# Squares kept as a pair of tiles, attention column groups on alternating PSUM halves, and a TensorE loop written out, in a decoder layer step

## The reference, cut to what matters

```python
x = x + 0.5 * swiglu(rmsnorm(x, g_ffn1), w_ffn1_in, w_ffn1_out)
h = rmsnorm(x, g_mix);  p = h @ w_in          # q, k, v of attention and GLA, gates
a  = rms(dilated_attention(...)) * g_att_out   # 16 heads x 64
gg = rms(gated_linear_attention(...)) * g_gla_out * silu(r_g)
x = x + concat(a, gg) @ w_out
x = x + 0.5 * swiglu(rmsnorm(x, g_ffn2), w_ffn2_in, w_ffn2_out)
y = rmsnorm(x, g_final)
# rmsnorm(x, g) = x * rsqrt(mean(x*x, features) + eps) * g
```

## Time and profile before

| | |
|---|---|
| median of 3 runs | 2145.38 us |
| lowest, highest | 2140.80, 2151.92 us |
| span of the profiled execution | 2142.6 us |
| PE busy | 2075.4 us, 97% |
| DVE busy | 1201.3 us, 56% |
| ACT busy | 881.7 us, 41% |
| POOL busy | 151.1 us, 7% |
| HBM traffic | 180 GB/s over the span |

### The profile page before, as it was taken

One profiled execution on the slowest core, in us unless ns is written; L12 is line 12 of the kernel. 1 busy time (PEld: TensorE's weight loads), 2 busy tenths in 40 slices (PEclk: granted clock), 3 DMA queues, 4 the chain that ended last, 5 costly groups with the idle time before them and its releaser, 6 DMA issues.

```text
span 2142.6 us, 40469 instructions
## 1 busy us (share of the span) xinstructions
PE 2075.4 (97%) x16651; PEld 2043.7 (95%) x16651; DVE 1201.3 (56%) x1300; ACT 881.7 (41%) x986; POOL 151.1 (7%) x93
## 2 busy tenths in 40 slices
PE   8999999999999999999988799999999999999997
PEld 7999999999999999999977799999999999999997
DVE  6555554554454545655698967655555545544443
ACT  5433434434343435433345534434344343433332
POOL 0000000000000001005342450000000000000000
PEclk9999999999999999999999899999999999999998
DMA  5665565665555465448975464555655555555553
GB/s 192 181 183 177 166 193 179 179 182 177 181 179 172 158 198 151 140 129 291 314 242 171 132 207 157 177 179 170 191 178 179 183 177 176 174 190 178 176 174 104
DMA packets 199868, 387.57 MB, mean 181 GB/s; under 512 B 14474, under 2 KB 22868, under 8 KB 199492
## 3 DMA queue, kind: packets, MB, share of 16 engines
q1 hardware_dynamic: 193312, 377.80, 57.0%
q10 hardware_dynamic: 5796, 6.53, 0.9%
q0 software_dynamic: 656, 1.74, 0.2%
HBM read 376.91 MB, written 9.11 MB: 180 GB/s over the span
## 4 chain that ended last, share of the span: by engine, by line
PE 84%; DVE 10%; ACT 2%; issue 2%; DMA 1%; POOL 0%; ACTq 0%; SPq 0%; DVEq 0%
PE g L575 27%; PE g L576 27%; PE g L577 26%; DVE wl L1376 3%; DVE t_buf L1401 1%; ACT wh L989 1%; DVE xl L1411 1%; PE g L778 0%; DVE dif L1560 0%; DMA raw<-in_w_out_dram 0%; DVE am L1583 0%; DVE sm L1633 0%; DVE sm L1635 0%; DVE gl L1740 0%; DMA bcast<-rows_q 0%
## 5 line engine op out<-in xcount | busy, mean ns | idle before, releaser
L1376 DVE TENSOR_TENSOR wl<-raw,wh 128x1024 fp32r<-128x1024 f32 x658 | 810.5, 1242 | 791.9 <-ACT wh L989 791.7
L989 ACT ACTIVATE wh<-raw 128x1024 fp32r<-128x1024 f32 x658 | 689.8, 1055 | 882.4 <-PE g L577 835.7
L575 PE MATMUL g<-xh,wh 128*128 128x264 f32 x3584 | 1031.4, 288 | 15.8 <-DVE va L1520 4.7
L576 PE MATMUL g<-xl,wh 128*128 128x264 f32 x3584 | 1024.1, 286 | 0.0
L577 PE MATMUL g<-xh,wl 128*128 128x264 f32 x3584 | 1023.7, 286 | 0.0
L575 PEld LDWEIGHTS g<-xh,wh 128*128 128x128 f32 x3584 | 681.5, 190 | 22.3 <-DVE wl L1376 15.7
L576 PEld LDWEIGHTS g<-xl,wh 128*128 128x128 f32 x3584 | 680.4, 190 | 0.2
L577 PEld LDWEIGHTS g<-xh,wl 128*128 128x128 f32 x3584 | 678.7, 189 | 0.0
L575 PE MATMUL g<-uh,wh 128*128 128x264 f32 x1408 | 401.2, 285 | 3.3 <-issue 2.6
L576 PE MATMUL g<-ul,wh 128*128 128x264 f32 x1408 | 400.6, 284 | 0.0
L577 PE MATMUL g<-uh,wl 128*128 128x264 f32 x1408 | 400.4, 284 | 0.0
(11 more groups left out here) (231 smaller groups left out, 1187.6 us busy)
## 6 DMA issues: line engine op xcount, KB each, us to landing
raw<-in_w_ffn_in_dram SPq DMA_DIRECT2D x352, 512.0 KB, 4.3
raw<-in_w_ffn_out_dram SPq DMA_DIRECT2D x176, 512.0 KB, 4.3
raw<-in_w_in_dram SPq DMA_DIRECT2D x96, 512.0 KB, 4.0
raw<-in_w_out_dram SPq DMA_DIRECT2D x32, 512.0 KB, 5.6
stream<-in_state_gla_dram SPq DMA_DIRECT2D x8, 512.0 KB, 5.1
bcast<-rows_v SPq DMA_DIRECT2D x8, 512.0 KB, 7.1
out_dram<-stream ACTq DMA_DIRECT2D x8, 512.0 KB, 6.7
stream<-in_cache_att_k_dram SPq DMA_DIRECT2D x8, 512.0 KB, 6.5
```

Source lines behind the costliest of these rows:

```text
L575: pe.matmul(out(n), hi, a, start=first and k == 0, stop=False)
L576: pe.matmul(out(n), hi, b, start=False, stop=False)
L989: act.activation(dst, src, ACT.Copy).then_inc(hi_done, 1)
L1376: dve.tensor_tensor(dst, src, h.bitcast(F32), ALU.subtract).then_inc(lo_done, 1)
```

## The change

- **Squares.** ssq becomes a pair of tiles (2 x 264). add_squares adds tiles 0, 1 to tiles 2, 3 of s_buf (one add of 528 elements) and adds the result to ssq (another of 528). mean and the final sum run a matmul for each half of ssq into the same place.
- **Attention column groups.** Groups 0 and 2 go to g0, groups 1 and 3 to g1. DVE takes a whole group with one instruction of 1056 elements, after PE's last matmul of the group. PE waits for the take of the group two back; before group 1 it waits until all side steps are done with g1. att_taken counts the takes. FFN2-in's first chunk waits for three takes, the matmul for its mean for four.
- **FFN1-out on PE** is written out for all 88 chunks. SP, ACT and DVE keep their loops.
- **smult** moves to a place that is free only later, so its load moves on POOL from the start to the end of the GLA state stores, ahead of the loads of mult and mask.

```diff
-                pe.matmul(g1[:, 0, 0:T], ones[:, 1, :].to_broadcast([P, P]), ssq[:, :], start=True,
+                pe.matmul(g1[:, 0, 0:T], ones[:, 1, :].to_broadcast([P, P]), ssq[:, 0, :], start=True, stop=False)
+                pe.matmul(g1[:, 0, 0:T], ones[:, 1, :].to_broadcast([P, P]), ssq[:, 1, :], start=False,
                           stop=True).then_inc(done, 1)
...
             def final_read(n):
-                pe.wait_ge(proj_new, MIX_TILES - CN_T + n + 1)
+                pe.wait_ge(att_taken, FO_BLOCKS - 1)
...
-                                for b in range(4):
-                                    pe.wait_ge(free[b], USES[b])
+                                pe.wait_ge(att_taken, FO_BLOCKS)
...
-            with pe.Fori(0, FO_BLOCKS // 2) as i:
-                for k in range(2 * FO_CH):
-                    b, j = k // FO_CH, k % FO_CH
...
+            for k in range(FO_BLOCKS * FO_CH):
+                q, j = k // FO_CH, k % FO_CH
+                if j == 0:
+                    pe.wait_ge((gate_in, up_in)[q % 2], FI_BLOCKS)
+                    pe.wait_ge(x_new, q + 3)
+                ffn_out_chunk(0, FO1 + k, q, j, (FO1 + k) % RING)
...
+                    if kind == "att" and m == 1 and j == 0:
+                        for b in range(4):
+                            pe.wait_ge(free[b], USES[b])
+                    if kind == "att" and m >= 2 and j == 0:
+                        pe.wait_ge(att_taken, m - 1)
...
-                    multiply(c, c % RING, rhs, lambda t: g0[:, t, 0:T], j == 0, last,
-                             bank_read if j == 0 else None, last)
+                    g = g1 if kind == "att" and m % 2 else g0
+                    multiply(c, c % RING, rhs, lambda t: g[:, t, 0:T], j == 0, last,
+                             bank_read if j == 0 and not (kind == "att" and m) else None,
+                             last and kind != "att")
...
-                mm = pe.matmul(g0[0:n, 3, half:half + 1], ssq[:, cols], ones[:, 1, :], start=True,
+                pe.matmul(g0[0:n, 3, half:half + 1], ssq[:, 0, cols], ones[:, 1, :], start=True, stop=False,
+                          skip_group_check=True)
+                mm = pe.matmul(g0[0:n, 3, half:half + 1], ssq[:, 1, cols], ones[:, 1, :], start=False,
                                stop=True, skip_group_check=True)
...
-                dve.tensor_reduce(t_buf[:, 0, :], s_buf[:, :, :].rearrange("p k t -> p t k"), AX_X,
-                                  ALU.add).then_inc(sq_part, 1)
+                dve.tensor_tensor(t_buf[:, 0:2, :], s_buf[:, 0:2, :], s_buf[:, 2:4, :], ALU.add).then_inc(sq_part, 1)
                 dve.wait_ge(sq_part, nth + 1)
-                dve.tensor_tensor(ssq[:, :], ssq[:, :], t_buf[:, 0, :], ALU.add).then_inc(ssq_new, 1)
+                dve.tensor_tensor(ssq[:, :, :], ssq[:, :, :], t_buf[:, 0:2, :], ALU.add).then_inc(ssq_new, 1)
...
+            def take_group(m, last_c):
+                dve.wait_ge(used, last_c + 1 + RING)
+                dve.tensor_tensor(t_buf[:, :, :], groups[m % 2][:, :, 0:T], wide(asq[:, :]),
+                                  ALU.mult).then_inc(att_taken, 1)
+                dve.wait_ge(att_taken, m + 1)
+                xq = x[:, 4 * m:4 * m + 4, :]
+                dve.tensor_tensor(xq, t_buf[:, :, :], xq, ALU.add).then_inc(x_new, 1)
...
-            pool.dma_start(smult[:, :], c_smult).then_inc(sconst_in, 16)
...
             pool.wait_ge(sfin_out, 64)
+            pool.dma_start(smult[:, :], c_smult).then_inc(sconst_in, 16)
             pool.dma_start(mult[:, :], c_mult).then_inc(attc_in, 16)
```

More of the change, by code:

```diff
@@ L96, in block_tiles @@
             before[kind, m] = n
-            n += CN_T
+            n += CN_T if kind != "att" else 0
     return before, n
@@ L274, in layer_step @@
         eps = sb("eps", [1])
-        ssq = sb("ssq", [T])
+        ssq = sb("ssq", [2, T])
         rstd = sb("rstd", [T])
@@ L284, in layer_step @@
         sm_s = sb("sm_s", [257])
-        smult = sb("smult", [257])
         pt_s = sb("pt_s", [2, H_ATT, TS])
@@ L331, in layer_step @@
         prod = at("prod", u_at + (4 * AT_T + 2 * H_GLA + AT_T) * T * 4, [448])
+        smult = at("smult", u_at + (4 * AT_T + 2 * H_GLA + AT_T) * T * 4 + 1792, [257])
         rows = at("rows", s_start, [2, 512])
@@ L403, in layer_step @@
         ath_new, atl_new = sem("ath_new"), sem("atl_new")
-        asq_new, arstd_new = sem("asq_new"), sem("arstd_new")
+        asq_new, arstd_new, att_taken = sem("asq_new"), sem("arstd_new"), sem("att_taken")
         stored = sem("stored")
@@ L1417, in clear_squares @@
             def clear_squares():
-                link(dve.memset(ssq[:, :], 0.0))
+                link(dve.memset(ssq[:, :, :], 0.0))
             def factor(nth):
@@ L1500, in _ @@
                         x_low(2 * i + (4 + b), 2 * i + b, 1)
+            def take_group(m, last_c):
[5 more added lines that the diff above has]
+                dve.tensor_tensor(xq, t_buf[:, :, :], xq, ALU.add).then_inc(x_new, 1)
             def take_tiles(n, kind, m, last_c):
+                if kind == "att":
+                    take_group(m, last_c)
+                    return
                 b0 = TILES_BEFORE[kind, m]
@@ L1521, in take_tiles @@
                         a.then_inc(proj_new, 1)
-                    elif kind == "gla":
+                    else:
                         xt = x[:, 4 * m + t, :]
                         dve.tensor_tensor(xt, src, xt, ALU.add).then_inc(proj_new, 1)
[L1525 to L1531, removed]
             def lowrank(_):
```

## The result

| | before | after |
|---|---|---|
| median of four runs, us | 2143.09 (2140.44 to 2151.92) | 2127.22 (2125.79 to 2128.75) |
| ratio, 95% interval | 1 | 0.9917 [0.9901, 0.9932] |
| span of the profiled execution, us | 2142.64 | 2124.05 |

The account below looks back on a forecast made before the run. PE, busy for 97% of the span, was taken as the bound, so time is won only where it stands still. Terms -2.8 - 2.2 - 1.0 - 4.2 + 1.35 + 0.1 = -8.8 us gave 2136.6 us; range 2130 to 2145.5.

Parts of the forecast that it names:

- The loop: Middle of PE's FFN1-out: the gap is the loop's jump back and goes when written out, -2.8 us.
- Rival C: FFN1-out: the 2.64 us wait is a fetch at that place, not the jump, and stays; -6.0, 2139.4 us; chance 0.10.
- D: FFN1-out: written-out PE code isn't fed fast enough; 0.1 us a chunk eats the gain, 2163 at 0.3; chance 0.05.
- The start: Near 35.74 us: shorter squares bring low half 4 earlier, PE's stall goes; -2.2 us with ACT's root.
- The root's part: At the start: ACT's root, just late at PE's eighth chunk, is ready earlier; -0.2 us.
- Squares in FFN1-out: Two low-half stalls of 0.35 + 0.16 us at FFN1-out boundaries go; -1.0 us.
- Rival B: Squares: the adds cost what they replace, 1.26 us each; no gain, 2145 us; chance 0.10.
- Attention: Attention column groups: DVE's turn falls from 13.22 to 11.9 us and still sets the pace; -4.2 us.
- Rival A: Attention: DVE falls off the path, adds at 0.68, turns under 11.7 us; -11 us, 2134; chance 0.17.
- The means: Three times PE runs a second fp32 matmul over 264 columns; +0.45 us each, +1.35 in all.
- The end: Last squares shorten DVE by 0.95 us, six added one-column pass records cost 1.1; +0.1 us.
- The mixer: Stage between FFN1-out and attention w_out: forecast +0.45 us.

Follow-up runs that it names:

- same: The kernel before with nothing edited, run for a second profile: 2145.19 us, ratio 1.0002.
- loop_only: The kernel before with only PE's FFN1-out loop written out: 2139.12 us, ratio 0.9977.
- attention_only: The kernel before with only the attention groups on alternating halves and the single take; squares and loop as before: 2145.32 us, ratio 1.0005.
- start_reduce: The changed kernel with the first four sets of squares summed by the old reduce: 2133.12 us, ratio 0.9943 to the kernel before.
- squares_only: The kernel before with only the squares as a pair and smult's move; takes and loop as before: 2136.40 us, ratio 0.9967.
- keep_jump: The changed kernel with PE's old loop in FFN1-out: 2137.89 us, ratio 0.9962 to the kernel before.
- full_again: The changed kernel run once more, nothing further edited: 2128.28 us, ratio 0.9915 to the kernel before.
- busy_delay: The changed kernel with twelve unused fp32 matmuls of 264 columns on PE ahead of the mixer: 2134.31 us, ratio 0.9952 to the kernel before.
- code_shift: The changed kernel with 128 semaphore increments ahead of PE's first instruction, shifting the code behind: 2145.11 us, ratio 1.0005 to the kernel before.
- wait_no_jump: The changed kernel, loop written out, with PE made to wait before group 2 of FFN1-out: 2134.47 us, ratio 0.9951 to the kernel before.

## Why the prediction was wrong

- **The loop, forecast -2.8: the step that failed on size.** The gap was the jump back, as said: in every kernel with PE's loop it is there (2.64 to 2.91 us), and in none without it, save where a wait was put. Rival C is out, and so is D: the pitch in the written-out loop is 50.00/411 = 0.122 us. But the step priced a stall as idle time only. Behind it the clock is at its lower level in the five other profiles that keep the loop, and that stretch takes 68.9 to 69.0 us against 64.5, some 4.5 more. The one profile read for the forecast was the only one where the clock didn't fall. That 2.93 - 0.12 = 2.8 fits the 2.91 between the first two profiles is the luck of this execution; for the kernel it is 1.6 short. The prediction's ten jumps back in FFN1-in are nine, between the ten rounds of its loop; they show no gap.
- **The start, forecast -2.2: right in place, short in size, and for the same reason.** The stall at 35.74 went. But behind it the clock was at 0.66 from 36 to 41 us, against 1.00 after:

```profile
36.00:41.00 5.00, 5.00 (x31) 5.00 (x31) 4.96 (x4) 3.40 (x4) 0.00 (x0) 0.66 0.49 127
```

```profile
36.00:41.00 5.00, 5.00 (x40) 4.87 (x40) 4.24 (x6) 2.72 (x3) 0.00 (x0) 1.00 0.72 215
```

  PE reaches the matmul of the mean at 43.15 before and at 39.59 after, 3.6 us earlier:

```profile
43.15 0.61 PE L586 MATMUL g<-ssq,ones 128*128 128x264 f32 x2
```

```profile
39.59 0.61 PE L586 MATMUL g<-ssq,ones 128*128 128x264 f32 x2
```

  2.0 of it are the stall, as forecast, and 1.6 the slow stretch, which the sum had at nothing. The second pass of the mean takes 0.45 back, and 3.1 is left. The root's part, put at -0.2, was nothing between these two profiles: neither shows PE waiting for it. The other executions with the reduce at the start (same, loop_only, attention_only, start_reduce) have no slow stretch there; PE waits 1.6 to 1.8 us for ACT's root instead, because the load that ACT's rounding ahead of it waits for came later: the rounding starts at 48.03 in same and at 46.78 before. Their first gate comes at 52.9 to 53.2, against 49.0 to 50.3 in the changed kernel. So about as much was lost each time, in one of two ways, and the forecast had one row to see it in.
- **Squares in FFN1-out, forecast -1.0:** two boundaries by 0.60 are -1.2, and the adds took 0.70 and 0.75 us. Rival B is out.
- **Attention, forecast -4.2, with the mean -3.75:** measured -4.24. The turn of 11.9 and the reason, DVE's turn as the bound, hold. How the edits share it was not as the sum had it: the sum took the 3 x 0.19 of the takes and the 1.15 of each set of squares together. squares_only shows that the squares alone bring 3.9 us; the single takes on alternating halves add 0.4 to that, and by themselves nothing. Rival A (turns under 11.7) is out: the turns are 11.9. Its own terms add up to -10.3 us, not to -11.
- **The means, forecast +0.45 each:** the two passes are 0.44 apart and the next matmul comes 0.25 behind the second, so 0.25 to 0.45; near enough.
- **The end, forecast +0.1:** 17.47 before, 17.1 to 17.4 in most changed kernels, 16.6 to 16.7 in the profile of after and in keep_jump and squares_only. The 1.1 us for the six one-column passes was read in a stretch where the clock stood at 0.50. At that clock the twelve now take 1.97 us up to the transposes (full_again) against 1.07 before; in the three profiles where it stayed up, 1.16 (after). Right for the lower clock, 0.9 too dear for the higher.
- **The mixer, forecast only +0.45: the step that failed outright, and its cause stays open in part.** The sum let nothing but the second mean pass change there, and took the rest of the stage as fixed. Between the first two profiles it became 6.2 us shorter. Of its instructions only that pass and smult's load (on POOL, ahead of mult and mask) are changed, and loop_only, which has neither, has the short mixer too. Six profiles with PE's loop kept took 466.3 to 470.9 us, mean 468.9; six with it written out and no work added right ahead of the mixer 463.2 to 465.0, mean 464.2. Part of the difference is the clock. From the first take of kg to the first of qg all thirteen profiles take 34.9 us where the clock stays at 1.00 and 35.9 where it falls once; before, then after (length, PE's busy time and matmuls, granted clock, DMA share, GB/s):

```profile
826.00:862.00 36.00, 35.70 (x267) 0.95 0.50 148
```

```profile
819.00:854.00 35.00, 34.46 (x267) 1.00 0.48 150
```

  It falls there in five of the six profiles with the loop and in one of the six without. From the takes of the second column group of w_out's gla half to those of the third it is the same: 13.9 us, and 15.3 to 15.5 where the clock falls, in four of the six and one of the six. These two places make about 1.4 of the 4.8 us. The means of the whole loss, 17.1 and 14.2, would make 2.9, but the loss doesn't go by the kernel (17.1 in after, whose mixer took 463.7). Why the clock falls in one execution and not in the next is not shown. The windows between the mixer's two takes of rg, where PE waits long for DVE, show one place where the length changes (before, then after):

```profile
1176.00:1228.00 52.00, 40.90 (x274) 36.62 (x274) 49.31 (x75) 31.62 (x46) 28.21 (x12) 0.90 0.45 142
```

```profile
1166.00:1215.00 49.00, 39.72 (x274) 35.29 (x274) 47.69 (x76) 31.84 (x47) 28.15 (x12) 0.90 0.49 151
```

  PE has 274 matmuls in both; it is busy 1.2 us less and idle 1.8 less after. But this stretch is short (49.2) in busy_delay too, and long (51.5) in code_shift, so it isn't one place that decides. A stall in FFN1-out (wait_no_jump) is out as the cause.

  The medians warn against reading more from one mixer each. As an estimate, take from each profiled mixer what its execution was above the median (last column of the table), as if all of that scatter were the mixer's: the kernels with the loop come to 467.8 to 469.8 us, those without it to 463.4 to 465.9, busy_delay among the short ones with 465.5, and code_shift among the long ones with 467.9. That keeps the loop's share and turns the two tests of its cause around. So neither the moment at which PE reaches the mixer nor the place of its code is shown to be the cause, and neither is ruled out; several profiles of each kernel would be needed.

By medians and ratios the loop is worth about 10 us in the changed kernel, 4.5 in FFN1-out and 5 to 6 in the mixer, but only 5 to 6 in the kernel before, 3.7 of them in FFN1-out; the squares are worth some 7, the alternating halves nothing that could be told. The three parts alone add up to 11 us, the change gains 18. Of the 7 between, 0.8 (the jump's stretch) and 0.4 (attention) are explained; the rest isn't, and is about what the intervals of the four ratios leave open together. The forecast's mechanisms account for about -13 once sized by the runs (start -3.1, boundaries -1.2, jump -4.5, attention with its mean -4.24, the other mean +0.25), and the mixer for most of the rest.

## What to carry to other kernels

Price a stall of PE of some microseconds with the slow stretch behind it, and look at the granted clock behind it in more than one execution: a single profile can show the cheap case. Where two engines take turns, find whose whole turn is the bound before working on the wait that the profile names; attention_only removed every one of those waits and gained nothing. In a stage with many side steps, a few microseconds can come or go without an edit in it, so keep that scatter in the range. Before a profile is taken for its kernel, compare the profiled execution's own time with the median: here 3 us were enough to reverse what two tests seemed to say.

## What was not expected of the hardware

- Behind a gap of 2.6 to 3.7 us PE's granted clock was 0.50 for about 3 us (nearly 6 behind the longest) in every profiled execution with such a gap in FFN1-out but one, and matmuls of 264 columns started 0.22 us apart instead of 0.122.
- 128 semaphore increments on PE put off its first work by some 14 us (its first idle time 20.5 us instead of 6.3). That is 0.11 us each at least, and 0.16 if they ran from the span's start, while PE would have waited for its data anyway; the profile doesn't show them.
- The mixer, with nearly the same instructions in all kernels, took from 463.2 to 470.9 us in thirteen profiled executions, and the clock fell at other points of its work from one to the next.
